# Where the moving operands of split-weight products lie, relative to the weights

## What is computed

```python
def squared_relu_mlp(h, w_up, w_down):
    a = jax.nn.relu(h @ w_up)
    return (a * a) @ w_down
...
for i in range(DEPTH):                        # first block
    hn = rmsnorm(x, attn_norm_g[i])
    mix, q_cross = mla_mixer(hn, ...) if i % 2 == 0 else swa_mixer(hn, ...)
    cross = memory_cross_attention(q_cross, mem_n, w_mem_kv[i])
    x = x + jnp.concatenate([mix, cross], axis=-1) @ w_o[i]
    x = x + squared_relu_mlp(rmsnorm(x, mlp_norm_g[i]), mlp_w_up[i], mlp_w_down[i])
...
x = x + g_m[:, None, :] * (y @ w_out)         # both layers of the second block
hf = modulate(rms_norm(x, ffn_norm), sh_f, sc_f)
x = x + g_f[:, None, :] * ((silu(hf @ w_gate) * (hf @ w_up)) @ w_down)
```

## Time and profile before

| | |
|---|---|
| median of 3 runs | 1195.02 us (1194.58 to 1195.56) |
| the profiled execution | 1194.61 us |
| its span | 1193.0 us |
| PE busy, share of the span | 1179.1 us, 99% |
| VectorE, ScalarE, GpSimd busy | 74%, 53%, 8% |
| granted TensorE clock | 1.00 |

### The profile page before, as it was taken

One profiled execution on the slowest core, in us unless ns is written; L12 is line 12 of the kernel. 1 busy time (PEld: TensorE's weight loads), 2 busy tenths in 40 slices (PEclk: granted clock), 3 DMA queues, 4 the chain that ended last, 5 costly groups with the idle time before them and its releaser, 6 DMA issues.

```text
span 1193.0 us, 22907 instructions
## 1 busy us (share of the span) xinstructions
PE 1179.1 (99%) x9549; PEld 1143.3 (96%) x9549; DVE 882.9 (74%) x1177; ACT 635.1 (53%) x853; POOL 98.4 (8%) x147
## 2 busy tenths in 40 slices
PE   8999999999999999999999999999999999999998
PEld 8999999999998999999999999999988779999998
DVE  5876778878766778778789887887677657866543
ACT  6558576633447566633558554333556655543332
POOL 0000001110034000111100001111000000000000
PEclk9999999999999999999999999999999999999999
DMA  8452577887662576778743658867746505576352
GB/s 312 150 177 72 177 249 250 297 299 245 229 230 72 178 249 231 283 290 283 261 161 135 200 157 296 278 237 277 272 143 246 176 21 165 186 250 207 130 194 84
DMA packets 150059, 248.96 MB, mean 209 GB/s; under 512 B 5553, under 2 KB 80922, under 8 KB 149978
## 3 DMA queue, kind: packets, MB, share of 16 engines
q1 hardware_dynamic: 135858, 197.17, 48.8%
q0 software_dynamic: 13952, 50.60, 11.5%
q10 hardware_dynamic: 168, 0.04, 0.0%
HBM read 246.74 MB, written 1.05 MB: 208 GB/s over the span
## 4 chain that ended last, share of the span: by engine, by line
PE 92%; DVE 1%; issue 0%; POOL 0%; ACT 0%; DVEq 0%
PE ps L2157 28%; PE ps L2159 27%; PE ps L2158 27%; PE ps L2441 2%; PE ps L2307 1%; PE ps L2754 1%; PE ps L2423 1%; PE ps L2728 1%; PE ps L2410 1%; PE ps L2770 1%; PE ps L2242 0%; PE ps L2409 0%; DVE w_lo L1262 0%; PE ps L2755 0%; PE ps L2732 0%
## 5 line engine op out<-in xcount | busy, mean ns | idle before, releaser
L1262 DVE TENSOR_TENSOR w_lo<-raw,w_hi 128x2048 fp32r<-128x2048 f32 (+4 forms) x196 | 412.9, 2145 | 93.8 <-ACT w_hi L747 93.6
L747 ACT ACTIVATE w_hi<-raw 128x2048 fp32r<-128x2048 f32 (+4 forms) x196 | 341.9, 1790 | 162.0 <-PE ps L2159 162.0
L2157 PE MATMUL ps<-h_both,w_hi 128*128 128x256 f32 (+1 forms) x1296 | 367.9, 284 | 2.6 <-DVE xT L1466 1.5
L2158 PE MATMUL ps<-h_both,w_hi 128*128 128x256 f32 (+1 forms) x1296 | 366.6, 283 | 0.0
L2159 PE MATMUL ps<-h_both,w_lo 128*128 128x256 f32 (+1 forms) x1296 | 366.6, 283 | 0.0
L2157 PEld LDWEIGHTS ps<-h_both,w_hi 128*128 128x128 f32 (+1 forms) x1296 | 247.9, 191 | 3.6 <-issue 3.3
L2158 PEld LDWEIGHTS ps<-h_both,w_hi 128*128 128x128 f32 (+1 forms) x1296 | 248.0, 191 | 0.1
L2159 PEld LDWEIGHTS ps<-h_both,w_lo 128*128 128x128 f32 (+1 forms) x1296 | 248.0, 191 | 0.0
L2157 PE MATMUL ps<-a_both,w_hi 128*128 128x256 f32 x864 | 239.0, 277 | 0.0
L2158 PE MATMUL ps<-a_both,w_hi 128*128 128x256 f32 x864 | 238.5, 276 | 0.0
L2159 PE MATMUL ps<-a_both,w_lo 128*128 128x256 f32 x864 | 238.5, 276 | 0.0
(11 more groups left out here) (423 smaller groups left out, 1812.9 us busy)
## 6 DMA issues: line engine op xcount, KB each, us to landing
ada_raw<-in_l_ada_w POOLq DMA_DIRECT2D x96, 512.0 KB, 7.0
raw<-in_mlp_w_up SPq DMA_DIRECT2D x32, 1024.0 KB, 7.0
raw<-in_mlp_w_down SPq DMA_DIRECT2D x32, 1024.0 KB, 6.8
raw<-in_l_ffn_w_gate SPq DMA_DIRECT2D x22, 1024.0 KB, 5.4
raw<-in_l_ffn_w_up SPq DMA_DIRECT2D x22, 1024.0 KB, 9.2
raw<-in_l_ffn_w_down SPq DMA_DIRECT2D x16, 768.0 KB, 5.7
raw<-in_l_w_qkv SPq DMA_DIRECT2D x12, 1024.0 KB, 6.4
raw<-in_l_w_in SPq DMA_DIRECT2D x10, 1024.0 KB, 6.4
```

What stands on the lines that cost most here:

```text
L747: nc.scalar.activation(w_hi[:, s.slot, cut], raw[:, s.slot, cut], ACT.Copy).then_inc(split_hi, 1)
L1262: nc.vector.tensor_tensor(w_lo[:, s.slot, cut], raw[:, s.slot, cut], w_hi[:, s.slot, cut].bitcast(F32), ALU.subtract).then_inc(split_lo, 1)
L2157: nc.tensor.matmul(to, sh, mh, start=first, stop=False, skip_group_check=True)
L2158: nc.tensor.matmul(to, sh, ml, start=False, stop=False, skip_group_check=True)
```

## The change

It alters addresses only. `line_h` (256 bytes) becomes `quadrant_sum` alone (128 bytes), and `negsink` gets a tile behind the arena. A filler `line_b` of 64 bytes is allocated behind `gqk`. So `h_wide` and `h_both` start 128 bytes earlier, and the arena 64 bytes earlier. Within the arena, `l_lo` moves from word 2064 to word 2048. No instruction, wait or DMA is added or removed; some read or write other addresses.

```diff
-        line_h = sb("line_h", [P, 64])
-        quadrant_sum, negsink = line_h[:, 0:32], line_h[:, 32:32 + SWA_HEADS]
+        quadrant_sum = sb("quadrant_sum", [P, 32])
         h_wide = sb("h_wide", [P, 2, KD, T + 2], F32R)
...
         gqk = sb("gqk", [P, 1])
+        sb("line_b", [P, 16])
         ada_part = sb("ada_part", [P, ADA_GROUPS, 16])
...
         sink = sb("sink", [P, SWA_HEADS])
+        negsink = sb("negsink", [P, SWA_HEADS])
...
         l_hi = at("l_hi", 0, [P, KD, T], F32R)
-        l_lo = at("l_lo", 2064, [P, KD, T], F32R)
+        l_lo = at("l_lo", 2048, [P, KD, T], F32R)
...
-                nc.vector.tensor_scalar(negsink, sink[:, :], -1.0, None, ALU.mult)
+                nc.vector.tensor_scalar(negsink[:, :], sink[:, :], -1.0, None, ALU.mult)
...
-            nc.vector.tensor_reduce(quadrant_sum, ident[:, :].rearrange("p (q m) -> p m q", q=4), AX.X, ALU.add).then_inc(quadrants_ready, 1)
+            nc.vector.tensor_reduce(quadrant_sum[:, :], ident[:, :].rearrange("p (q m) -> p m q", q=4), AX.X, ALU.add).then_inc(quadrants_ready, 1)
...
-                    ins = nc.tensor.matmul(ps[32 * j:32 * (j + 1), NORM_BANK, T:T + n], quadrant_sum, part[:, :, j],
+                    ins = nc.tensor.matmul(ps[32 * j:32 * (j + 1), NORM_BANK, T:T + n], quadrant_sum[:, :], part[:, :, j],
```

## The result

The changed kernel took 1207.18 us (median of 4 runs, 1206.5 to 1207.41) against 1195.29 us (median of 4, 1194.58 to 1195.95): +11.9 us, ratio 1.0099 with a 95% interval of 1.0084 to 1.0113. It is slower, by more than a measurement can miss. The forecast was 1214.2.

What follows compares the result with a forecast made beforehand. TensorE, 99% busy, was taken as the bound, through matmul spacing. Terms 17.1 + 2.5 + 0.4 + 0.2 - 0.5 - 0.5 = +19.2 us on 1194.6 gave 1213.8, or 1214.2 on the median's scale; range 1207 to 1221, chance 0.55.

Steps and rivals of the forecast that it cites:

- What bounds the kernel: TensorE busy 99% of 1193.0 us; three split-weight matmul lines hold 82.6% of the chain, so their spacing counts nearly in full.
- Placement against the ring decides: Split-weight matmuls: moving operand's address relative to the weight buffers sets spacing, 113.3 ns at 192, 119.9 at 256.
- the rival by which placement was not the cause: The cost belongs to who writes `h_both`, or to nothing that moves: 1195 us, chance 0.05.
- D: Each operand's byte address in its partition, less that of weight buffer `w_hi`, taken modulo 512.
- The duration as gauge: A matmul's duration stands for its start-to-start spacing: 276 ns for 113.3, 283 ns for 119.9.
- 120.0 ns at D = 128: Spacing taken for the new placement from six starts in `w_in`; made `a_both` +17.1 us, `o_hi` and `o_lo` +2.5.
- `h_both` as weights, 0: The 336 matmuls using `h_both` as weights, moved from 256 to 128, were to cost 0 us.
- `l`, `m`, `u`, `h_wide`: Smaller matmul groups: +0.4, +0.2, -0.5 and -0.5 us forecast, -0.4 together.
- 128 is free: Rival: distance 128 costs nothing, `h_both` gains 25.5 us, -31.8 us in all, 1163 us; chance 0.30.
- worse than 256: Rival: distance 128 gives 121.6 ns, +32.5 us in all, 1227 us; chance 0.07.
- In between, near 118: Rival: spacing near 118, `a` and `o` +14.0, `h_both` -8.0, +6 us in all, 1201 us; chance 0.03.
- Adding up: Whole kernel: time is a sum of matmul starts, so per-matmul changes times counts give +19.2 us.

Runs made afterwards that it cites:

- a128_only: Kernel before with only the arena moved, from D = 192 to 128, `h_both` left at 256: 1209.99 us, ratio 1.0121.
- abs128: Kernel before with three small tiles allocated ahead of `raw`, so ring and operands all lie 128 bytes higher, distances unchanged: 1195.23 us, ratio 1.0000.
- h448: Kernel before with `negmax` allocated ahead of `h_wide`, so `h_both` lies at D = 448, `a_both` at 192: 1179.4 us, ratio 0.9889.
- both192: Changed kernel with `h_both` and the arena at D = 192 instead of 128: 1179.2 us, ratio 0.9849 to the kernel before.
- h128_only: Kernel before with only `h_both` moved, from D = 256 to 128, the arena left at 192: 1195.51 us, ratio 0.9996.

## Why the prediction was right, point by point

- **What bounds the kernel: right.** PE stayed 99% busy, the three lines hold 82.7% of the chain, no other engine took up or gave back more than a few tenths of a microsecond of it.
- **Placement against the ring decides: right, and shown.** Moving only the operands changes their spacing (a128_only), moving ring and operands together does not (abs128). That refutes the rival by which placement was not the cause. But D counts modulo 256, not 512 (h448). The prediction's "a quarter as long", of the weight load with 32 columns, is not what the trace records: 108 ns against 192 in the trace before. That the weights' reading is where the cost arises stays argued.
- **The duration as gauge: right.** 276, 281 and 283 ns stood for 113.3, 118.6 and 120.0 in every kernel. A group's mean hides the two spacings of 192, though (278 in both192); there only windows tell them apart.
- **120.0 ns at D = 128: the term that was mis-sized.** It was read from six starts in `w_in`, where D changes with every third matmul, and the single slow duration of the earlier trace rows backed it. In a steady stream it is 118.6. So `a_both` and `o` were put 1.3 ns too dear (19.6 us against 15.7), and `h_both`, costed at 0, gained 5.0 us, which is the larger part of the miss. The bounds taken, 113.3 and 121.6, hold it.
- **`h_both` as weights, 0: wrong in size.** +1.3 us. No row of before showed these forms at 128, and they were set to their cost at 256.
- **`l`, `m`, `u`, `h_wide`: small, as said, but of the other sign.** Together -0.4 was forecast and about +0.8 measured; the mean durations moved by 2 ns or less in most groups, and by 4 in one of `m` as weights (279 to 283).
- **The forecast against the rivals.** "128 is free" asked for under 117.2 ns, "worse than 256" for 121.6; the windows exclude both. "In between, near 118" was given 0.03 and 1201 us. By spacing it is what happened, and the time, 1207.2, lies midway between it and the forecast, at the edge of the forecast's own range, 1207 to 1221; that it fell inside, by 0.2 us, is luck. The sign was right since under either the 2976 matmuls that lose 5 ns or more outweigh the 3864 that gain 1 to 2. But the chances gave too little to a value between the two known ones.
- **Adding up: right, from spacings that were measured.** The terms give 12.0 of 11.9 us in the changed kernel, 15.7 of 15.6 in a128_only's profiled execution and 1.5 of 1.3 in h128_only's. What does not hold in general is the step from distance to spacing: at 192 there are two (h128_only, both192), and a forecast for that placement needs the stretches that fall into 117.8.

## What to carry to other kernels

If PE is busy throughout, count equal-shaped matmuls in equal windows, operand by operand; where the counts differ, vary the distance between moving operand and weights in small steps, both operands together, and read the settled value in a long steady stream, never in a passage where the distance itself changes. A kernel whose runs of the same code scatter by several microseconds may hold two spacings, so look at windows of each stage in more than one run before an edit is blamed or credited. And price a placement for every role of a tile, as moving operand and as weights.

## What the runs showed of the hardware that was not expected

- Matmuls of one form (128x128 weights, 256 columns), at one clock, settle near 113.3, 117.4, 117.8, 118.4, 118.6 or 120.0 ns. Hardly a block lies elsewhere, and which values are open depends on the distance modulo 256 (five distances tried, in steps of 32 bytes; what lies between was not tried).
- At 192 there are two. The stream was seen to change over where it is interrupted, by a gap or by a matmul of another form, and kept its spacing in between, in both192 from 14 us (968 to 982) to the whole second MLP (390 to 588). Before an experiment shows it, one sees only a kernel with runs 9 us apart.
- At 192 a matmul with 32-column weights, put into a stream that ran at 117.8 ns, was followed by 113.3 in four of four places; behind a gap of over 400 ns in six of nine. At 128 it changes nothing.
- Why these distances and these values, the trace does not tell: it shows starts and ends, not the reads in memory. That the reads of moving operand and next weights meet is argued from the 32-column rows and from the distance alone. The Trainium skill, SBUF — State Buffer, section "A bandwidth-pool intuition that's wrong (but worth ruling out)", gives TensorE a second independent read port for LDWEIGHTS (the sentence on the shared port pair that the prediction quotes stands in the section before it, "SBUF: two separate sides"), which would leave no room for any effect of distance; the measurement decides, with 28.0 us between two placements of the same instructions, the changed kernel's and both192's. The Trainium skill, TensorE: Matmul & The Clock Gate, section "Back-to-back issue gap", says that in a stream of weight loads and matmuls the spacing "is set by *both* ops"; that agrees with these runs, but the page has one spacing for each size, where here one size has six.
